# Three edits on a one-core hybrid block: the delta stage's spread and state order, a stick step that takes two heads, and the last output tile in two halves of columns

## The chip, the cores and the metric

The kernel runs on one core of one Trainium2 chip. The metric is the device time of one execution in microseconds. Of the kernel before there are three timed runs and one profiled execution. All times below are of that profiled execution, counted from the start of its span, unless something else is said.

## The reference

The program is one forward pass over a sequence of 512 positions with 1024 channels: a first block (a gated delta layer, a feed-forward layer, a banded attention layer, a second feed-forward layer, a final norm) and a second block with two branches that are gated, added and projected. Everything is float32. The parts that matter here:

```
# delta layer, per head, chunks of 64 (the kernel takes chunks of 128, four of them)
m = where(strict, (k*beta) @ k.T * decay, 0)
uw = triangular_solve(m + eye, concat([v*beta, k*beta*exp(gcum)]))     # the "solve"
v_new = u - w @ state;  o = q_dec @ state + attn_qk @ v_new
state = state * chunk_decay + k_end.T @ v_new                          # the "state" steps
o = rmsnorm(o, out_norm_w) * silu(z);  out = o @ w_out

# stick-breaking attention of the second block: 8 heads of 64, per block of queries
z = q @ k.T * dh**-0.5
log_keep = where(before, log_sigmoid(-z), 0)
log_stick = reverse_cumsum(log_keep) - log_keep
w = where(before, exp(log_sigmoid(z) + log_stick), 0);  o = w @ v      # and later o * silu(gate)

# spatial gating: 8 groups of 64 channels, chunks of 128 positions
mixed = einsum('gts,bnsgc->bntgc', w, vn) + b_s;  out = u * mixed

# the end
h = h + merged @ w_out_2;  result = rmsnorm(h, final_norm_g_2)
```

## The kernel before

Activations lie transposed: 128 channels on the partitions, 512 positions along the columns, eight such tiles for the 1024 channels (`h`). A dense product of one 128-channel output tile is 24 matmuls of 512 columns: for each of eight channel tiles k, the weights' high part with the input's high part (line 590), with its low part (line 591), and the weights' low part with the high part (line 592); in the delta stage these are called strips (line 616). The parts come about so: SyncE loads a weight tile into one of four raw slots, ScalarE casts it to the high part (`cast`, line 1152), VectorE subtracts that from the raw tile for the low part (`low`, line 1682) and so frees the slot. TensorE waits for the low part of a tile before its first matmul. The order on each engine is written out by hand, with a counting semaphore for each kind of event; every engine executes its list in order.

**Delta stage**, eight heads, one loop body each (`delta`, on TensorE, ScalarE and VectorE). A body has two halves. In the first (`levels`) TensorE multiplies a block system ("spread", line 721), ScalarE copies it out (`system_of`, line 1305), VectorE solves it (`solve`, lines 1852 to 1865) and transposes the result to `tn` (line 1872); then come four levels (products at lines 739 to 743 and, after VectorE's mask `xm`, joins at lines 756 to 760; VectorE's work in the gaps is `between(0)` to `between(7)`), with strips of tiles 2 and 3 of head i in between. In the second half four state steps t follow (lines 790 to 810; VectorE's `rr`, line 1946, and `state`, line 1961; ScalarE's `vn`, line 1330), with strips of tiles 0 and 1 of head i + 1 in between. After them VectorE normalizes k, takes the Gram product (`gram`, ending with the system's operand at line 1844), scales the outputs of head i (`outputs_of`, lines 1994 and 1997), takes the z tile of the next head and solves its system. The convolution taps (`conv_newest` on ScalarE, `conv_older` on VectorE) and silus of head i + 1 are spread over the body.

**Stick stage.** Four pairs of heads i; for each pair, each head e and each key block k (3 down to 0, with (4 - k) * 128 query columns) there is one unit, 32 in all. TensorE: logits (line 1017, full 128-row contraction: the q of one head has zeros in the other head's 64 rows), suffix sums (line 1042), values (line 1029, full 128-column weights: a head's v has zeros in the other's 64 columns). ScalarE: copy from PSUM (line 1552), exp and ln of -|z| (1557, 1559), exp of the log weight (1564). VectorE: |z| (2218), subtraction of the suffix sums (2223), mask (2226), max and add (2232), keep mask (2234), the last rows of the sum so far (2237). A step s holds the logits of unit s, the suffix sum of unit s - 2, the values of unit s - 4, and three dense pieces (a piece is one k of a tile, three matmuls) of the next pair's k, v, q tiles or of the gating stage's first tiles. 96 pieces lie inside the loop.

**Gating stage.** Four bodies; in each eight small products at line 1067 write 64 output partitions: first the four chunks of one group to partitions 0 to 63, then the four of the other to 64 to 127.

**The end.** The out stage has two bodies of four tiles. After the last tile VectorE adds it to `h` (2039), ScalarE squares it (1407), TensorE sums over channels with two f32 matmuls (1139, 1141), ScalarE takes ln and exp (1196, 1198), VectorE multiplies the eight tiles by gain and 1/rms (2385), and SyncE stores each (494).

## Time and profile before

| | us |
|---|---|
| median of three runs | 1811.98 (1811.54 to 1814.11) |
| the profiled execution | 1811.66 |
| its span, first to last instruction | 1810.0 |
| TensorE busy / VectorE busy / ScalarE busy | 1770.5 / 1188.5 / 843.6 |
| delta stage, roughly | 45 to 370 |
| stick loop | 1434 to 1558 |
| gating stage | 1558 to 1640 |
| out stage and end | 1745 to 1810 |

TensorE's granted clock is 0.999 over the span, its 2.4 GHz level. The shown durations of matmuls run from first column in to last result out and overlap; what a matmul costs in a full row of them is the time from its start to the next one's start. An f32 matmul appears as two records of equal shape; the dense products, on operands split in two parts, as one record each.

### The profile page before, as it was taken

The numbers are of one execution on the slowest core, as the hardware profiler recorded it, in microseconds if no ns is written. First come the engines' busy times: TensorE is split into PE (matmuls) and PEld (weight loads), VectorE is DVE, ScalarE is ACT, GpSimd is POOL, SyncE is SP. The second block draws the span as 40 slices with busy tenths as digits, with TensorE's granted clock in tenths as the row PEclk, the third lists the DMA queues.
The fourth block names the chain that finished last, engine by engine and source line by source line (L and its number), as shares of the span: only waits on it lengthen the run. The fifth ranks groups of instructions, "written<-read, shape, count | busy, mean of one in ns | idle before, by whom it ended". The sixth has DMA issues, their size and how long they took to land.

```text
span 1810.0 us, 23712 instructions
## 1 busy us (share of the span) xinstructions
PE 1770.5 (98%) x8122; PEld 1403.4 (78%) x8122; DVE 1188.5 (66%) x1948; ACT 843.6 (47%) x1360; POOL 35.6 (2%) x65
## 2 busy tenths in 40 slices
PE   9999999999999999999999999999999999999997
PEld 6777777678888888888887788888887876777885
DVE  7888888657777743367777677776433588765444
ACT  6554454444444432267777444444323455643222
POOL 1000000000000000000000000000001000000000
PEclk9999999999999999999999999999999999999999
DMA  5521212122222242143332222222321312323221
GB/s 201 161 69 63 65 58 60 46 82 93 93 93 93 70 144 96 62 122 100 111 100 81 94 93 93 93 93 89 117 96 52 105 36 70 97 73 99 98 93 58
DMA packets 44825, 163.27 MB, mean 90 GB/s; under 512 B 5873, under 2 KB 6148, under 8 KB 44768
## 3 DMA queue, kind: packets, MB, share of 16 engines
q1 hardware_dynamic: 39872, 148.00, 24.4%
q0 software_dynamic: 4464, 14.47, 2.9%
q8 instruction: 32, 0.52, 0.1%
q14 instruction: 25, 0.20, 0.0%
q10 hardware_dynamic: 432, 0.07, 0.0%
HBM read 155.89 MB, written 6.63 MB: 90 GB/s over the span
## 4 chain that ended last, share of the span: by engine, by line
PE 90%; DVE 5%; ACT 2%; issue 1%; DMA 0%; SPq 0%; DVEq 0%; ACTq 0%
PE acc L590 23%; PE acc L591 23%; PE acc L592 23%; PE acc L616 7%; DVE wsplit L1682 1%; PE pb L739 1%; PE pc L756 1%; PE pd L1029 1%; PE pa L1017 1%; ACT wsplit L1152 1%; PE pa L591 1%; PE pa L590 1%; PE pa L592 1%; PE pa L715 1%; PE pd L967 1%
## 5 line engine op out<-in xcount | busy, mean ns | idle before, releaser
L590 PE MATMUL acc<-xhi,wsplit 128*128 128x512 f32 x1200 | 496.6, 414 | 1.1 <-DVE at_vs L2114 1.0
L1152 ACT ACTIVATE wsplit<-wraw 128x1024 fp32r<-128x1024 f32 (+1 forms) x252 | 276.2, 1097 | 435.6 <-PE acc L592 407.9
L591 PE MATMUL acc<-xlo,wsplit 128*128 128x512 f32 x1200 | 475.5, 396 | 0.0
L592 PE MATMUL acc<-xhi,wsplit 128*128 128x512 f32 x1200 | 475.3, 396 | 0.0
L1682 DVE TENSOR_TENSOR wsplit<-wraw,wsplit 128x1024 fp32r<-128x1024 f32 (+1 forms) x249 | 316.8, 1273 | 142.4 <-ACT wsplit L1152 141.4
L590 PEld LDWEIGHTS acc<-xhi,wsplit 128*128 128x128 f32 x1200 | 226.1, 188 | 60.2 <-issue 5.3
L591 PEld LDWEIGHTS acc<-xlo,wsplit 128*128 128x128 f32 x1200 | 226.4, 189 | 55.4 <-issue 4.3
L592 PEld LDWEIGHTS acc<-xhi,wsplit 128*128 128x128 f32 x1200 | 225.8, 188 | 54.7
L616 PE MATMUL acc<-xhi,wsplit 128*128 128x512 f32 x464 | 159.1, 413 | 5.8 <-DVE wsplit L1682 5.7
L591 PE MATMUL acc<-hid_lo,wsplit 128*128 128x512 f32 x352 | 139.6, 396 | 0.0
L590 PE MATMUL acc<-hid_hi,wsplit 128*128 128x512 f32 x352 | 139.5, 396 | 0.0
L592 PE MATMUL acc<-hid_hi,wsplit 128*128 128x512 f32 x352 | 139.5, 396 | 0.0
L616 PEld LDWEIGHTS acc<-xhi,wsplit 128*128 128x128 f32 x464 | 83.9, 189 | 26.4 <-issue 9.8
L2073 DVE TENSOR_TENSOR tmp<-acc,rstd 128x512 f32<-128x512 f32 x88 | 60.5, 688 | 65.5 <-PE acc L592 57.7
L2039 DVE TENSOR_TENSOR h<-h,acc 128x512 f32<-128x512 f32 (+1 forms) x38 | 26.1, 687 | 112.4 <-PE acc L592 112.3
L616 PE MATMUL acc<-xlo,wsplit 128*128 128x512 f32 x232 | 98.8, 426 | 0.0
L1441 ACT ACTIVATE hid_hi<-fy 128x512 f32 (+1 forms) x44 | 27.8, 633 | 110.0 <-DVE fy L2084 110.0
L1434 ACT ACTIVATE fy<-tmp,vec 128x512 f32<-128x512 f32 x88 | 71.1, 809 | 17.0 <-DVE tmp L2073 17.0
L592 PEld LDWEIGHTS acc<-hid_hi,wsplit 128*128 128x128 f32 x352 | 66.3, 188 | 16.2
L590 PEld LDWEIGHTS acc<-hid_hi,wsplit 128*128 128x128 f32 x352 | 66.3, 188 | 16.2
L591 PEld LDWEIGHTS acc<-hid_lo,wsplit 128*128 128x128 f32 x352 | 66.3, 188 | 16.2
L2079 DVE SCALAR_TENSOR_TENSOR fy<-tmp,vec,fy 128x510 f32<-128x510 f32 x88 | 66.0, 750 | 12.0 <-DVE fy L2076 3.1
(386 smaller groups left out, 2611.2 us busy)
## 6 DMA issues: line engine op xcount, KB each, us to landing
wraw<-w SPq DMA_DIRECT2D x220, 512.0 KB, 3.3
wraw<-w SPq DMA_DIRECT2D x32, 704.0 KB, 4.1
bias_dram<-ext_dram POOLq DMA_DIRECT2D x1, 4096.0 KB, 23.2
bias<-bias_dram POOLq DMA_DIRECT2D x16, 256.0 KB, 3.0
at_ks<-at_ks SPq DMA_DIRECT2D x16, 256.0 KB, 2.9
crow<-row_dram POOLq DMA_DIRECT2D x8, 256.0 KB, 3.9
brow<-row_dram POOLq DMA_DIRECT2D x8, 256.0 KB, 4.5
outT<-h SPq DMA_DIRECT2D x8, 256.0 KB, 2.1
```

What stands on the lines that cost most here:

```text
L590: mm(out, whi[:, k, :], a[:, x_at + k, :], start=(k == first), stop=False)
L591: mm(out, whi[:, k, :], b[:, x_at + k, :], start=False, stop=False)
L592: m = mm(out, wlo[:, k, :], a[:, x_at + k, :], start=False, stop=(k == last))
L616: d = mm(bank(s, i, j), w[:, k, :], x[:, k, :], start=(m == 0), stop=(m == 3 * KD - 1))
L715: m = mm(pa[:, t // 2, (t % 2) * 2 * P:(t % 2 + 1) * 2 * P], kn[:, t * P:t * P + P], kq[:, t, :, :].rearrange("p a q -> p (a q)"), start=T ...
L1152: A(split(s, i, j, 0), raw(s, j), ACT.Copy).then_inc(w_hi_ready, 1)
L1434: A(fy[:, j, :], tmp[:, j % 2, :], ACT.Identity, scale=w[:, g, f, 2:3], bias=wb[:, g, f, :]).then_inc(ev("ffn_newest"), 1)
L1441: A(hid_hi[:, f, :], fy[:, j, :], ACT.Copy).then_inc(ev("hid_hi_ready"), 1)
L1682: tt_(split(s, i, j, 1), raw(s, j), split(s, i, j, 0).bitcast(F32), ALU.subtract).then_inc(w_lo_ready, 1)
L2039: tt_(h[:, i * per + m, :], h[:, i * per + m, :], bank(s, i, j) if s in rolling else acc[:, m % 2, :], ALU.add).then_inc(acc_free, 1 if s. ...
L2073: tt_(tmp[:, j % 2, :], acc[:, j % 2, :], rstd[:], ALU.mult).then_inc(acc_free, 1)
L2079: stt(fy[:, j, 2:S], tmp[:, j % 2, 0:S - 2], w[:, g, f, 0:1], fy[:, j, 2:S], ALU.mult, ALU.add).then_inc(ev("ffn_conv"), 1)
```

## The change

- **Delta, TensorE:** `spread(i + 1)` moves from the start of the next body to the end of this one, six strips ahead of its end (for the last head the order of TensorE stays).
- **Delta, VectorE:** `outputs_of` is cut in two; its second multiply (`outputs_normed`) moves behind `solve(i + 1)`. `low(i + 1, 0)` moves from gap 7 to gap 6, the last tap of tile 2 from gap 6 to gap 7; the taps of tile 3 and `exponent` move later in the state steps.
- **Delta, ScalarE:** the cast of the outputs (`output_hi`) moves into the next body, behind the first weight cast; `square_k` and `conv_newest(3)` move behind `vn_of(0)`. Head 0 is unrolled.
- **Stick, all engines:** a step takes both heads of a block: 16 blocks instead of 32 units. Logits are two 64-row products into two PSUM banks, values two 64-column products into two partition halves; `sk_q` and `sk_vt` lose their zero halves, and GpSimd its memsets. ScalarE and VectorE operations span both heads. |z| moves to ScalarE; the mask is added before |z|, so the keep mask is gone. Dense pieces: six a step up to step 10, then the rest over seven steps.
- **Gating, TensorE:** the eight products alternate between the two halves.
- **End:** the last tile is computed in two halves of 256 columns; the norm's sum, root, multiplies and stores are done by halves, the multiplies of four and three tiles in one instruction. The gain is multiplied in earlier, tile by tile. The loops of the out stage are unrolled.

```diff
# TensorE, delta
             def levels(i, last):
-                if last:
-                    out_pieces(*OUT_SPREAD)
-                spread(i)
...
-                    fill((3 * KD if last_qkv else 2 * 3 * KD) - done[0])
+                    whole = 3 * KD if last_qkv else 2 * 3 * KD
+                    fill(whole - done[0] - (0 if last_qkv else AFTER_SPREAD))
+                    if last_qkv:
+                        out_pieces(*OUT_SPREAD)
+                    spread(i + 1)
+                    fill(whole - done[0])
# VectorE, delta
-                    if gap in (4, 5, 6):
+                    if gap in (4, 5):
                         conv_older(i, 2, i + 1, (gap - 3,))
+                    if gap == 6:
+                        low(s, i + 1, 0)
                     if gap == 7:
-                        low(s, i + 1, 0)
+                        conv_older(i, 2, i + 1, (3,))
                         take(i, 3)
...
-                if not last:
-                    conv_older(i, 3, i + 1, (1,))
...
                         if t == 1 and not last:
-                            conv_older(i, 3, i + 1, (3,))
-                            exponent(i + 1)
+                            conv_older(i, 3, i + 1, (2, 3))
...
                         if t == 0 and not last:
-                            conv_older(i, 3, i + 1, (2,))
+                            conv_older(i, 3, i + 1, (1,))
+                        if t == 1 and not last:
+                            exponent(i + 1)
...
-                    outputs_of(i)
-                    dve.wait_ge(ev("oy_ready"), i + 1)
+                    outputs_gated(i)
+                    dve.wait_ge(ev("on_ready"), i + 1)
                     take(i + 1, 0)
                     solve(i + 1)
+                    outputs_normed(i)
# ScalarE, delta
                 if not last:
                     cast_ahead(s, i, 1, False)
+                if not (isinstance(i, int) and i == 0):
+                    output_hi(i - 1)
+                if not last:
                     conv_newest(1, i + 1, i)
...
-                    square_k(i)
-                    conv_newest(3, i + 1, i)
...
                 vn_of(0)
                 if not last:
+                    square_k(i)
+                    conv_newest(3, i + 1, i)
# TensorE, stick
+                        for e in range(2):
+                            own = slice(64 * e, 64 * e + 64)
+                            m = mm(pa[:, e, 0:(4 - k) * P], sk_k[own, i % 2, k * P:k * P + P], sk_q[own, i % 2, k * P:S],
+                                   start=True, stop=True)
+                        m.then_inc(ev("logits_done"), 1)
+                    a = done + (upto(step) - done + 1) // 2
+                    c = a + (upto(step) - done) // 6
+                    dense(done, a)
+                    if 1 <= step < blocks + 1:
+                        k = 3 - (step - 1) % NC
+                        pe.wait_ge(ev("sp_ready"), step)
...
+                        for e in range(2):
+                            m = mm(pbc[:, e, 0:(4 - k) * P], order[:, O_SUF, :], sp[:, e, SEG[k]:SEG[k] + (4 - k) * P],
+                                   start=True, stop=True)
+                        m.then_inc(ev("suffix_done"), 1)
+                    dense(a, c)
+                    if step >= 2:
+                        i, k = (step - 2) // NC, 3 - (step - 2) % NC
+                        pe.wait_ge(ev("sw_ready"), step - 1)
...
+                        for c0, c1 in zip(cuts, cuts[1:]):
+                            for e in range(2):
+                                own = slice(64 * e, 64 * e + 64)
+                                m = mm(pd[own, c0 * P:c1 * P], sk_vt[:, i % 2, k, own],
+                                       sw[:, e, SEG[k] + (c0 - k) * P:SEG[k] + (c1 - k) * P], start=(k == 3), stop=(k == 0 and c1 == NC))
# ScalarE, stick: order of a step
+                    if step < blocks:
...
+                        A(zs[:, :, g], pa[:, :, 0:(4 - k) * P], ACT.Copy).then_inc(ev("zs_ready"), 1)
+                    if 2 <= step < blocks + 2:
...
+                        A(sw[:, :, g], zs[:, :, g], ACT.Exp).then_inc(ev("sw_ready"), 1)
+                    if step < blocks:
...
+                        A(sw[:, :, g], zs[:, :, g], ACT.Abs).then_inc(ev("z_abs"), 1)
+                        A(sw[:, :, g], sw[:, :, g], ACT.Exp, scale=-1.0).then_inc(ev("z_exp"), 1)
+                        A(sw[:, :, g], sw[:, :, g], ACT.Ln, bias=1.0).then_inc(ev("z_ln"), 1)
+                    if 0 < i < SBP and v == 0:
+                        turned_v(i)
+                        cast_ahead(s, i, 2, i == SBP - 1)
+                    if i < SBP - 1 and v in (1, 3):
+                        cast_ahead(s, i + 1, v // 2, i + 1 == SBP - 1)
# VectorE, stick: order of a step
+                        tt_(zs[:, :, g], zs[:, :, g], pbc[:, :, 0:(4 - k) * P], ALU.subtract).then_inc(ev("drest"), 1)
...
+                        x = stt(sp[:, :, g], zs[:, :, g], 0.0, sw[:, :, g], ALU.max, ALU.add)
...
+                            x = stt(sp[LAST:P, :, later], pbc[0:32, :, 0:(3 - k) * P], cst[LAST:P, C_ID, LAST:LAST + 1],
+                                    sp[LAST:P, :, later], ALU.mult, ALU.add)
...
+                        tt_(zs[:, :, own], zs[:, :, own], order[:, O_NEGD, :].unsqueeze(1).to_broadcast([P, 2, P]), ALU.add
+                            ).then_inc(ev("z_masked"), 1)
+                    if ahead and v == 3:
                         take(i + 1, 2)
...
+                    if ahead and v in (1, 2):
+                        take(i + 1, v - 1)
+                    if ahead and v in (2, 3):
+                        low_ahead(s, i + 1, v - 2, i + 1 == SBP - 1)
# TensorE, gating
-                    for e in range(2):
-                        for t in range(NC):
+                    for t in range(NC):
+                        for e in range(2):
# TensorE, end
+                product(s, j, acc[:, 1, 0:HALF], a, b, 0, KD).then_inc(acc_done, 1)
+                a, b = mg_hi[:, :, HALF:S], mg_lo[:, :, HALF:S]
+                product(s, j, pb[:, 0:HALF], a, b, 0, 5)
+                final_sum(0)
+                product(s, j, pb[:, 0:HALF], a, b, 5, KD).then_inc(acc_done, 1)
+                final_sum(1)
# VectorE, end
+                for k0, k1 in FINAL_PARTS:
+                    if k1 < KD:
+                        x = tt_(h[:, k0:k1, cols], h[:, k0:k1, cols], rstd[:, cols].unsqueeze(1).to_broadcast([P, k1 - k0, HALF]), ALU.mult)
+                    else:
+                        x = stt(h[:, k0, cols], h[:, k0, cols], vec[:, G_FIN2 + k0:G_FIN2 + k1], rstd[:, cols], ALU.mult, ALU.mult)
# SyncE, end; FINAL_PARTS = [(0, 4), (4, 7), (7, 8)]
+            for n in range(2):
+                for m, (k0, k1) in enumerate(FINAL_PARTS):
...
+                    sp.dma_start(outT[part], h[part]).then_inc(ev("stored"), 16)
```

## Rows read from the trace of the kernel before

**Rows 1.** The page's first part: busy us, share of the span, instructions of each engine.
```profile
PE 1770.5 (98%) x8122; PEld 1403.4 (78%) x8122; DVE 1188.5 (66%) x1948; ACT 843.6 (47%) x1360; POOL 35.6 (2%) x65
```
**Rows 2.** TensorE's waits: us in total, times, longest us.
```profile
PE acc L616 <- DVE wsplit L1682: 5.7, 7, 0.8
PE pb L739 <- DVE tn L1872: 5.7, 8, 1.0
```
**Rows 3.** Timeline of TensorE in one head: start us, duration us, instruction, idle before.
```profile
173.04 0.60 PE L721 MATMUL pa<-xm,cst 128*128 128x256 f32 x2
...
176.75 0.40 PE L616 MATMUL acc<-xlo,wsplit 128*128 128x512 f32 x1
177.89 1.16 PE L739 MATMUL pb<-tn,gd 128*128 128x128 f32 x8 [0.74 <-DVE tn L1872]
...
193.94 0.49 PE L616 MATMUL acc<-xhi,wsplit 128*128 128x512 f32 x1 [0.82 <-DVE wsplit L1682]
...
213.64 0.60 PE L721 MATMUL pa<-xm,cst 128*128 128x256 f32 x2
```
**Rows 4.** Timeline of VectorE in the same head.
```profile
174.11 0.31 DVE L1852 TENSOR_TENSOR st<-system 128x144 f32<-128x144 f32 x1 [0.56 <-ACT system L1305]
...
192.26 0.42 DVE L1937 COPY tt<-pd 64x256 f32<-64x256 f32 x1
...
195.42 0.75 DVE L1752 SCALAR_TENSOR_TENSOR ys<-tmp,vec,ys 128x511 f32<-128x511 f32 x1 [1.01 <-ACT ys L1235]
...
211.61 0.43 DVE L1844 TENSOR_TENSOR xm<-gdc,en 128x256 f32<-128x256 f32 x1
```
**Rows 5.** Timeline of TensorE: start, one step and end of the stick loop.
```profile
1434.27 0.60 PE L1003 MATMUL acc<-cst,sk_v 128*128 128x128 f32 x4
...
1488.38 1.02 PE L1017 MATMUL pa<-sk_q,sk_k 128*128 128x512 f32 x2
...
1489.47 0.39 PE L591 MATMUL acc<-xlo,wsplit 128*128 128x512 f32 x1
...
1558.39 0.60 PE L1054 MATMUL pb<-cst,gv 128*128 128x128 f32 x4
```
**Rows 6.** Groups by line and shape, 1430 to 1562 us: busy us, mean ns; idle before.
```profile
L1682 DVE TENSOR_TENSOR wsplit<-wraw,wsplit 128x1024 fp32r<-128x1024 f32 x13 | 15.9, 1225 | 0.6 <-ACT wsplit L1152 0.3
...
L1152 ACT ACTIVATE wsplit<-wraw 128x1024 fp32r<-128x1024 f32 x13 | 13.6, 1047 | 4.6 <-PE acc L592 4.6
...
L2218 DVE SCALAR_TENSOR_TENSOR sw<-zs 128x512 f32<-128x512 f32 x8 | 5.5, 692 | 1.8 <-ACT zs L1552 1.7
...
L1557 ACT ACTIVATE sw<-sw 128x512 f32<-128x512 f32 x8 | 5.0, 628 | 0.0
...
L2218 DVE SCALAR_TENSOR_TENSOR sw<-zs 128x128 f32<-128x128 f32 x8 | 2.3, 290 | 4.5 <-ACT zs L1552 4.5
```
**Rows 7.** Timeline of TensorE around one gating product.
```profile
1569.60 0.39 PE L591 MATMUL acc<-xlo,wsplit 128*128 128x512 f32 x1
1569.83 0.40 PE L592 MATMUL acc<-xhi,wsplit 128*128 128x512 f32 x1
1570.16 1.58 PE L1067 MATMUL pc<-wcur,xc 128*64 128x128 f32 x16
1571.67 0.50 PE L590 MATMUL acc<-xhi,wsplit 128*128 128x512 f32 x1
1572.00 0.40 PE L591 MATMUL acc<-xlo,wsplit 128*128 128x512 f32 x1
```
**Rows 8.** Line 1067 by windows: stretch, length, TensorE busy (records touching it), clock, DMA.
```profile
1570.90:1571.00 0.10, 0.10 (x7) 1.00 0.00 0
```
**Rows 9.** Timeline of VectorE at the end.
```profile
1797.98 0.69 DVE L2039 TENSOR_TENSOR h<-h,acc 128x512 f32<-128x512 f32 x1 [3.48 <-PE acc L592]
...
1801.99 5.39 DVE L2385 SCALAR_TENSOR_TENSOR h<-h,vec,rstd 128x512 f32<-128x512 f32 x8 [3.32 <-ACT rstd L1198]
```
**Rows 10.** The page's DMA issues: count, KB each, median us to landing.
```profile
outT<-h SPq DMA_DIRECT2D x8, 256.0 KB, 2.1
```

294 lines of the change are left out of this document (133 added, 161 removed).

## The prediction

> **What bounds the kernel now.** I read the page's busy list first: TensorE has work for 98% of the span, VectorE for 66% [rows 1]. So only three things can shorten the run: fewer TensorE column cycles, less waiting of TensorE, or a shorter tail behind its last product. Then the list of waits: almost all that TensorE waits for in the delta stage are two VectorE results, about 0.7 us a head each, the turned blocks tn ahead of line 739 and the low half of a weight tile ahead of line 616 [rows 2]. The timeline of one head (its period is 213.64 - 173.04 = 40.6 us) places them [rows 3]. A dense matmul takes 0.235 us from start to start [rows 7], so between 176.75 and 177.89 us 0.90 us are lost; the wait before 193.94 is shown as 0.82 and costs some 0.16 more by the same reading, 0.98. Next the stick stage: from 1434.27 to 1558.39 us, 124.1 us [rows 5]. It holds 96 dense pieces of three matmuls, 67.5 us; 96 f32 products for logits, suffix sums and values, each at 0.43 us a record of 512 columns, two records a matmul (two records and one dense step fill the 1.09 us from 1488.38 to 1489.47 [rows 5]): 32 head-blocks x 320 columns on average x 1.68 ns = 17.1 us per kind, 51.2 in all; transposes 1.8; rest, some 3.6 us, waits. It is TensorE's stage, though VectorE is close behind. Last the end: 12 us behind the last product [rows 9].
>
> **Delta: the spread six matmuls earlier, the outputs' last multiply behind the solve.** The spread for the next head now stands 6 x 0.235 = 1.41 us before the old place, at 212.23 us in a head where it stood at 213.64 [rows 3]. Its operand is finished at 211.61 + 0.43 = 212.04 [rows 4], so TensorE does not wait for it, with 0.2 us to spare. The solve waited 0.56 us for the copy of the spread [rows 4]; it now starts 1.4 us earlier, because one 0.69 us multiply is gone from before it. tn is then ready 0.5 us before TensorE wants it: the 0.90 us go. What comes late next is the moved multiply and the low half, ahead of the first level's mask on VectorE; by the same durations they end within 0.1 us of when its operand is there. I take nothing for it. Head 0's solve stays as it was, and the last head's spread keeps its place, so it is 6 heads x 0.90 = 5.4 us. The output cast on ScalarE now stands behind the next head's weight cast; behind it there waits only the newest tap of tile 1, whose input VectorE gives after the first level's mask, later than the cast ends. It costs nothing unless the moved multiply slips behind that mask; then all 0.69 us of it would show in each head.
>
> **Delta: the low half before the last join.** The 1.23 us subtraction goes from behind the copy at 192.26 [rows 4] into the gap before it; it ends at about 192.5, half a microsecond before TensorE's two strips of the next tile, and the copy is needed only after those. The 0.98 us go. In exchange one 0.75 us tap of tile 2 moves behind it, and its silu stands before the first vn on ScalarE: 0.1 us. The newest tap of tile 3 moves behind vn; VectorE, which waited 1.01 us for it before 195.42 [rows 4], gets it later and holds up rr by 0.15 to 0.3. Price 0.2, bounds 0 and 0.7 (all of that tap). Net 0.78 x 7 heads = 5.5 us. The two delta edits give 10.9, bounds 7 and 12.5.
>
> **Stick: two heads a step.** What is removed on VectorE (|z|, the keep mask, half of the instruction starts, one of two q multiplies) takes it from near 28 us a pair of heads to 18, each operation priced at its columns by rows 6; |z| goes to ScalarE, which stays near 19 us. Both are below TensorE's 30. Neither gain is on the path by itself.
>
> On TensorE the logits of two heads contract over 64 rows each, in different halves of the array, and the values go to different halves of the output partitions. Do these run at once? The trace has one such case: line 1067 writes partitions 0 to 63 eight times, then 64 to 127 eight times. 16 records of 0.107 us of columns should fill 1.71 us, but the next dense matmul starts 1.51 us after the first [rows 7], though it pays for two changes. And in the table by tenths of a microsecond seven records are in flight in the middle [rows 8], where a start every 0.107 us and a duration of 0.27 allow three or four: the second half of the array starts while the first still works. So column halves overlap, even out of program order. For row halves the trace shows nothing; the bounds are full overlap and none, and I take full overlap from that nearest row. Logits and values each go from 17.1 to 8.5 us: -17.1.
>
> The Trainium skill, "TensorE: Matmul & The Clock Gate" (section "The mechanism"), has matmuls start and end in strict program order. The measured overlap contradicts that for column halves; by that rule the two records of the second head would start only with the second of the first.
>
> The same excursion has a price. Line 1067 starts 0.33 us after the dense matmul before it, where 0.235 is usual, and behind it the second dense matmul comes 0.33 after the first [rows 7]: 0.19 us outside the group. Inside its 1.51 us I estimate 0.14 for a slow first record and the way back: 0.33 us in all. Full-array excursions (line 1017, rows 5) cost none. The change makes 32 excursions, two a block: +10.7 us, bounds 0.19 and 0.5 each, 6 and 16.
>
> The Trainium skill, "TensorEngine Tiling (Array Packing)" (section "Key Properties"), says that changing the tiling mode drains the engine; the trace agrees with its 0.33 us.
>
> Then the chain of one step. DVE's durations follow 0.16 us + 1.05 ns a column [rows 6], so both heads at 512 columns cost 1.23, at 384 0.95; ScalarE's likewise 1.08. Take the widest block (v = 3), TensorE's step beginning at 0: logits 1.2, copy to 2.4, exponential of an older block to 3.0, |z|, exp and ln to 6.3. Now ScalarE's weight cast (1.05 [rows 6]) to 7.3, for which VectorE's low half waits, to 8.6, and behind which stand the subtraction for the older block (9.6), this block's sum and its wrap-around rows, to 11.9. TensorE asks for it at 10.2: its step is 4.2 dense + 1.2 + 1.3 + 0.8 = 7.5, then 0.5 of logits and 2.1 dense. It stalls 1.7 us, in three of the four pairs: +5.1, bounds 0 (the low half is ready early) and 9. The waits at the end, 3.6 us, I leave. Sum: 124.1 - 17.1 + 10.7 + 5.1 = 122.8: only 1.3 us gained.
>
> **Gating, order of the eight products.** Alternating halves run from the start at one record in 0.109 us per half: 0.87 + 0.2 instead of 1.51: 0.44 x 4 = 1.8 us; bounds 0 and 2.6.
>
> **The end.** The last tile in halves costs TensorE nothing but the f32 sum (0.43 + 0.43 a half). Before, from the last addition at 1797.98 to the first final multiply at 1801.99 4.01 us pass, and the eight multiplies take 5.39 [rows 9]. After, the second half's addition stands at 1798.9, since the first half's sum (0.86) is put before its last nine products; the same chain at half the columns takes about 2.9 us, to 1801.8; the first half's multiplies (1.23 + 0.95 + 0.42) fit in between. The second half's three end at 1804.4 instead of 1807.4: 3.0. The seven extra multiplies by the gain lie in VectorE's idle time in the out stage. The stores now have 1 KB runs and fewer, larger pieces. 256 KB took 2.1 us to land [rows 10]; the last pieces come at 1 MB in 1.3 us, so I take 0.4 off: 2.6 us, bounds 0.5 and 3.2.
>
> **Sum.** 10.9 + 1.3 + 1.8 + 2.6 = 16.6. VectorE fills 86% of a shorter head afterwards, and ends that I put within 0.1 to 0.2 us of each other will not all hold; for that I take off 1.6. 1811.66 (the profiled execution, span 1810.0) - 15 = 1796.7; its median of three is 0.3 above, so 1797.0. About 0.2% (3.6 us) is what a measurement can tell from no change.
>
> **Rivals.**
> - Row halves don't overlap. For it: no row shows 64-row products. Against: rows 8 for columns. The logits keep 17.1 us: +8.5, of which about 2 fall into stalls that exist anyway: 1803.5. Chance 0.13.
> - Starts in program order. Then a head pair's four records take three slots: the logits save 4.3 instead of 8.5, the values (cut in two pieces) 5.6: +7.2, less 1 of stalls: 1803. Rows 7 and 8 speak against it. Chance 0.04. (It is the rule of the Trainium skill cited above.)
> - New waits eat half of the delta gain, because VectorE, not TensorE, then sets the head's period: +5.4: 1802.4. For it: 0.2 us margins; against: 14% idle VectorE. Chance 0.12.
> - Cheap excursions and a short chain: if the stall of 5.1 does not come and an excursion costs 0.25: -7.7: 1789.5. Chance 0.09.
> - Slower: the excursion is dearer for row halves. All other gains together are 15 us; 16 logits excursions decide from 0.33 + 15/16 = 1.3 us each. At 1.7 us, if each time the array had to run empty and two weight loads followed in series, +22: 1819. Nothing in the rows is near it. Chance 0.02.
> - The change doesn't do what it says (waits reappear one for one, stick as before): within 0.2%. Chance 0.02.
>
> The forecast keeps 0.58, own range 1793 to 1801. The whole range, 1790 to 1804, takes in the first three rivals. Faster by over 0.2%: 0.96, same 0.02, slower 0.02.
>
> **What will show it.** Right: no wait for tn at line 739 in heads 1 to 6 and none for a weight tile at 616; a head's period of 38.9 us; stick loop between 120 and 126 us with waits of TensorE for sp once in a pair; lines 1067's group under 1.1 us; pa's two halves starting together; last multiply ending near 1790. Wrong: second-head logits starting after the first's (row halves), a period still above 40 us (VectorE-bound), or stick below 117 (my stall is not there).

## The result and the profile after

The changed kernel takes 1793.74 us (median of four runs, 1793.58 to 1794.55); the kernel before, timed beside it on the same chip, 1811.88 (1811.54 to 1814.11). The ratio is 0.9899, with a 95% interval of 0.9886 to 0.9911: 18.1 us less. The forecast was 1797.0 with a range of 1790 to 1804. The profiled execution has a span of 1791.9 us; all times inside a run are counted from its start.

The first part of the page, as [rows 1], and TensorE's longest waits in the delta and stick stages and at the end, as [rows 2] (us in total, times, longest us):

```profile
PE 1761.8 (98%) x8174; PEld 1388.8 (78%) x8174; DVE 1153.6 (64%) x1826; ACT 845.8 (47%) x1311; POOL 34.4 (2%) x61
```
```profile
PE pbc L1029 <- DVE sp L2263: 4.5, 4, 1.8
...
PE pbc L792 <- DVE rr L1976: 1.1, 4, 0.4
PE pbc L1147 <- ACT tmp L1699: 1.1, 1, 1.1
PE pbc L733 <- DVE tn L1902: 1.0, 1, 1.0
```

The wait for a weight tile's low half (5.7 us in [rows 2]) is gone, and of the waits for tn only head 0's is left. A wait for sp, the tile that the suffix sums read, takes the first place; the list of before has none. The old stick loop had another:

```profile
PE pd L1029 <- ACT sw L1564: 2.5, 3, 1.0
```

It is gone too.

Where the 18.1 us come from, by the start of the stick loop (its first transpose, line 1003 before and 1002 now) and the stages behind it:

| stage | before | after | less |
|---|---|---|---|
| up to the stick loop | 1434.27 | 1422.23 | 12.0 |
| stick loop | 124.12 | 121.48 | 2.6 |
| gating product, each of 4 | 1.51 | 1.03 | 1.9 in all |
| from the last gating product's start to the end | 181.5 | 180.0 | 1.5 |

**Delta.** TensorE's timeline at two spreads one head apart: the period is 205.68 - 167.03 = 38.65 us, where [rows 3] gives 40.6.

```profile
166.79 0.40 PE L613 MATMUL acc<-xhi,wsplit 128*128 128x512 f32 x1
167.03 0.59 PE L718 MATMUL pa<-xm,cst 128*128 128x256 f32 x2
167.27 0.58 PE L613 MATMUL acc<-xhi,wsplit 128*128 128x512 f32 x1
167.69 0.40 PE L613 MATMUL acc<-xlo,wsplit 128*128 128x512 f32 x1
...
205.68 0.59 PE L718 MATMUL pa<-xm,cst 128*128 128x256 f32 x2
```

**Stick.** TensorE's timeline over the widest block of a pair and the first of the next, to be held against [rows 5]:

```profile
1471.11 0.40 PE L589 MATMUL acc<-xhi,wsplit 128*128 128x512 f32 x1
1471.44 1.13 PE L1017 MATMUL pa<-sk_q,sk_k 64*128 64x512 f32 x4
1472.50 0.50 PE L587 MATMUL acc<-xhi,wsplit 128*128 128x512 f32 x1
1472.84 0.40 PE L588 MATMUL acc<-xlo,wsplit 128*128 128x512 f32 x1
...
1481.81 0.39 PE L589 MATMUL acc<-xhi,wsplit 128*128 128x512 f32 x1
1483.28 1.98 PE L1029 MATMUL pbc<-sp,order 128*128 128x512 f32 x4 [1.08 <-DVE sp L2263]
```

The logits of two heads are four records of 512 columns, and the next dense matmul follows 1.06 us after the first of them. Full overlap of two row halves takes 0.85 for the columns (two records at 0.43). In the trace's records the four start at 1471.438, 1471.445, 1471.971 and 1471.978: two at a time, 0.007 us apart. The last line is a stall: from 1481.81 a dense matmul accounts for 0.23 of 1.47 us. The first matmuls behind the logits also lie 0.34 us apart instead of 0.235, as in [rows 7].

What holds sp up stands in VectorE's timeline of the same moment:

```profile
1474.91 0.69 DVE L2238 SCALAR_TENSOR_TENSOR sk_q<-acc,rstd 128x512 f32<-128x512 f32 x1 [0.81 <-PE acc L589]
1478.35 1.23 DVE L1712 TENSOR_TENSOR wsplit<-wraw,wsplit 128x1024 fp32r<-128x1024 f32 x1 [2.75 <-ACT wsplit L1170]
1479.49 0.68 DVE L2293 TENSOR_TENSOR ya_lo<-sk_o,ya_hi 128x512 fp32r<-128x512 f32 x1
1480.10 0.95 DVE L2253 TENSOR_TENSOR zs<-zs,pbc 128x768 f32<-128x768 f32 x1
1480.96 1.22 DVE L2258 SCALAR_TENSOR_TENSOR sp<-zs,sw 128x1024 f32<-128x1024 f32 x1
1482.21 1.01 DVE L2263 SCALAR_TENSOR_TENSOR sp<-pbc,cst,sp 32x768 f32<-32x768 f32 x1
```

VectorE stands 2.75 us at the low half (line 1712), waiting for ScalarE's cast, with four operations queued behind it; the last releases TensorE at 1483.2.

**Gating**, TensorE, against [rows 7]: the group of 16 records lasts 1.03 us to the next dense matmul instead of 1.51.

```profile
1555.47 1.09 PE L1071 MATMUL pbc<-wcur,xc 128*64 128x128 f32 x16
1556.50 0.51 PE L587 MATMUL acc<-xhi,wsplit 128*128 128x512 f32 x1
```

**The end**, VectorE, against [rows 9]: second half's addition, the first half's multiplies, the second half's.

```profile
1782.31 0.42 DVE L2419 TENSOR_TENSOR h<-h,pbc 128x256 f32<-128x256 f32 x1 [3.29 <-PE pbc L589]
1782.65 2.08 DVE L2427 TENSOR_TENSOR h<-h,rstd 128x1024 f32<-128x1024 f32 x2
...
1785.52 2.09 DVE L2427 TENSOR_TENSOR h<-h,rstd 128x1024 f32<-128x1024 f32 x2 [0.39 <-ACT rstd L1217]
1787.53 0.48 DVE L2429 SCALAR_TENSOR_TENSOR h<-h,vec,rstd 128x256 f32<-128x256 f32 x1
```

The last multiply ends at 1788.0, and the span 3.9 us later; before, 2.6 us lay between them (1801.99 + 5.39 = 1807.4 [rows 9], span 1810.0). In the kernel before the DMA engines were already full at that place. By window (last two columns: their share, GB/s), from the second multiply on:

```profile
1804.00:1809.00 5.00, 0.00 (x0) 0.00 (x0) 3.38 (x6) 0.00 (x0) 0.00 (x0) 0.57 1.02 381
```

### The profile page after: what moved, and what is told of

Read it like the earlier page. It is cut to its first block, busy times and chain, and to the rows that moved or that the text cites. A ratio compares the mean times of both kernels' runs of the same rounds, so it can differ in the third digit from the quotient of the medians.

```text
span 1791.9 us, 23591 instructions
## 1 busy us (share of the span) xinstructions
PE 1761.8 (98%) x8174; PEld 1388.8 (78%) x8174; DVE 1153.6 (64%) x1826; ACT 845.8 (47%) x1311; POOL 34.4 (2%) x61
## 4 chain that ended last, share of the span: by engine, by line
PE 91%; DVE 4%; ACT 3%; issue 1%; DMA 0%; SPq 0%; DVEq 0%; ACTq 0%
PE acc L587 23%; PE acc L588 23%; PE acc L589 23%; PE acc L613 8%; ACT wsplit L1170 1%; PE pbc L750 1%; PE pbc L954 1%; PE pbc L733 1%; PE pa L587 1%; PE pa L588 1%; PE pa L589 1%; DVE wsplit L1712 1%; PE pbc L1029 1%; PE pa L712 1%; PE pd L967 1%
## 5 line engine op out<-in xcount | busy, mean ns | idle before, releaser
L2077 DVE TENSOR_TENSOR h<-h,acc 128x512 f32<-128x512 f32 (+2 forms) x38 | 25.8, 680 | 107.2 <-PE acc L589 107.2
```

The lines of the kernel that those rows point to most:

```text
L2077: tt_(h[:, i * per + m, cols], h[:, i * per + m, cols], out, ALU.add).then_inc(acc_free, 1 if s.kc == KD else 2)
```

## The experiments

Twelve kernels ran, in three groups of four (e1 to e4, e5 to e8, e9 to e12), each group on another chip and timed beside the kernel before (1811.91, 1812.11 and 1812.39 us). The changed kernel had 1811.88 beside it. So a difference between kernels of different groups is known to some 0.5 us; measured against the kernel before of its own group, e7 is -0.24, e9 -0.29, e10 +2.76, e11 -0.60 and e12 +3.07. The loop is the stick loop of the profiled execution.

| run | base | median us (all runs) | against its base | loop starts | loop lasts |
|---|---|---|---|---|---|
| changed kernel | | 1793.74 (1793.58 to 1794.55) | | 1422.23 | 121.48 |
| e1_delta_back | changed | 1805.89 (1805.61 to 1807.11) | +12.15 | 1434.46 | 121.50 |
| e2_stick_back | changed | 1796.37 (1795.84 to 1796.47) | +2.63 | 1422.33 | 124.10 |
| e3_low_late | changed | 1799.48 (1799.20 to 1801.34) | +5.74 | 1429.97 | 121.50 |
| e4_spread_back | changed | 1800.75 (1800.59 to 1801.24) | +7.01 | 1428.71 | 122.67 |
| e5_low_behind_sp | changed | 1789.15 (1788.73 to 1789.31) | -4.59 | 1422.31 | 116.90 |
| e6_logits_whole | changed | 1797.01 (1796.81 to 1797.17) | +3.27 | 1422.19 | 124.90 |
| e7_store_out | changed | 1793.73 (1793.31 to 1795.40) | -0.01 | | |
| e8_gate_end_back | changed | 1797.16 (1796.93 to 1797.30) | +3.42 | 1422.32 | 121.47 |
| e9_finer_parts | changed | 1793.96 (1793.21 to 1795.06) | +0.22 | 1422.02 | 122.72 |
| e10_values_whole | e5 | 1792.19 (1791.68 to 1793.91) | +3.04 | 1421.83 | 120.10 |
| e11_best | e5 | 1788.83 (1788.55 to 1788.86) | -0.32 | 1422.31 | 116.73 |
| e12_two_visits | e5 | 1792.50 (1792.41 to 1794.06) | +3.35 | 1423.85 | 120.38 |

### The delta edit: whole, and its two pieces

**e1_delta_back** puts the three engines' old delta order back (spread at the head of `levels`, `low(s, i + 1, 0)` in gap 7, both outputs' multiplies ahead of the solve, the old order between the state's steps) and nothing else; it holds the two diffs below, on ScalarE the old places of the output cast, `square_k` and tile 3's newest tap, and, on VectorE (with the first of these taps back ahead of the state steps),

```
                         if t == 1 and not last:
-                            conv_older(i, 3, i + 1, (2, 3))
+                            conv_older(i, 3, i + 1, (3,))
+                            exponent(i + 1)
...
                         if t == 0 and not last:
-                            conv_older(i, 3, i + 1, (1,))
+                            conv_older(i, 3, i + 1, (2,))
```

> The changed kernel with the old delta order throughout (spread at the head of levels, the low part of strip 0 in the last gap of the levels, old order between the state's steps, o_hi taken in its own iteration); stick step, gating and end stay changed. Theory, the delta edit is a gain of its own in the 8-head loop and nothing behind it depends on it: the stick loop starts 12.0 us later (at 1434.3 instead of 1422.2), the stages behind it keep their lengths (121.5, 1.03 x4, 16.4), and the time is 1793.7 + 12.0 = 1805.8. Rival, part of the 12.0 came from the later stages' earlier loads or from the buffers: the stick loop starts less than 10 us later.

The loop starts at 1434.46, the time is +12.15, and the loop behind lasts 121.50. The theory holds: the delta edit is worth 12.1 us by itself, and nothing behind it hangs on it.

**e3_low_late**:

```
-                    if gap in (4, 5):
+                    if gap in (4, 5, 6):
                         conv_older(i, 2, i + 1, (gap - 3,))
-                    if gap == 6:
-                        low(s, i + 1, 0)
                     if gap == 7:
-                        conv_older(i, 2, i + 1, (3,))
+                        low(s, i + 1, 0)
                         take(i, 3)
```

> The changed kernel with one piece of the delta edit undone: in the levels, VectorE's low part of strip 0 goes back from the sixth gap (ahead of the last join's read) to the seventh (behind it), and the last convolution of q ahead of it. Theory, the low part released late cost TensorE 0.98 us a head before the first strip of the next head, and is worth its wait less 0.1: about 7 x 0.9 = 6.3 us more, 1800.0, and the wait on the low part at the strip (line 613) is back at about 1 us per head. Rival, the spread's shift and the new order between the state's steps already give the low part the time: under 2 us more, 1795.

+5.74, and the wait is back to the figure: TensorE's list has

```profile
PE acc L613 <- DVE wsplit L1712: 5.7, 7, 0.8
```

as in [rows 2]. (Its loop starts 7.7 us later in the profiled execution, because 1.9 us of that are lost ahead of the first spread: there the granted clock fell for some 3 us, as the last section shows. From the first spread to the last product of the output projection it is 5.8 us longer.)

**e4_spread_back** moves the spread and VectorE's last multiply of the output back:

```
     def levels(i, last):
+        if last: out_pieces(*OUT_SPREAD)
+        spread(i)
...
-        fill(whole - done[0] - (0 if last_qkv else AFTER_SPREAD))
-        ...
-        spread(i + 1)
-        fill(whole - done[0])
+        fill((3 * KD if last_qkv else 2 * 3 * KD) - done[0])
...
-        outputs_gated(i); take(i + 1, 0); solve(i + 1); outputs_normed(i)
+        outputs_of(i);    take(i + 1, 0); solve(i + 1)
```

> The changed kernel with the other piece of the delta edit undone: the spread matmul stands again at the head of levels, with nothing between it and the level's first product but that head's 14 strip matmuls, and VectorE multiplies the output by its norm ahead of the solve. Theory, the wait of 0.9 us on tn at the first level product is back, about 6 x 0.9 = 5.4 us, plus the 0.24 per head that the strips paid behind the spread, 1.7: 1799 to 1801. If both pieces add up, the rises of this run and of the run with the low part late sum to 12.0 within 1. Rival, one of the two waits covers the other: the two rises sum to under 9.

+7.01. TensorE's timeline of one head:

```profile
169.93 0.40 PE L613 MATMUL acc<-xhi,wsplit 128*128 128x512 f32 x1
170.16 0.60 PE L718 MATMUL pa<-xm,cst 128*128 128x256 f32 x2
170.72 0.50 PE L613 MATMUL acc<-xhi,wsplit 128*128 128x512 f32 x1
171.06 0.39 PE L613 MATMUL acc<-xlo,wsplit 128*128 128x512 f32 x1
...
173.87 0.40 PE L613 MATMUL acc<-xlo,wsplit 128*128 128x512 f32 x1
175.01 1.16 PE L736 MATMUL pbc<-tn,gd 128*128 128x128 f32 x8 [0.75 <-DVE tn L1899]
```

The 0.90 us ahead of the level product are back (175.01 - 173.87 - 0.24), and a second cost shows that the forecast had not read: from the spread to the second strip behind it 0.90 us pass here (170.16 to 171.06), and 0.66 in the changed kernel (167.03 to 167.69). That is 0.24 a head. 6 x (0.90 + 0.24) = 6.8. The two pieces add up to 12.75, 0.6 more than e1, which also puts the order between the state steps and ScalarE's order back; that third part has no run of its own. Where the 0.24 us come from is open. The tile that follows the spread is another (strips of tiles 2 and 3 before, of tiles 0 and 1 now), and the edge of the loop body stood right ahead of the spread and now lies among strips; no run changed either alone.

### The stick step

**e2_stick_back** takes the old stick code on all four engines, with its padded `sk_q` and `sk_vt`:

```
-                for step in range(blocks + 2):
+                for step in range(units + 4):
...
-                            m = mm(pa[:, e, 0:(4 - k) * P], sk_k[own, i % 2, k * P:k * P + P], sk_q[own, i % 2, k * P:S],
+                        mm(pa[:, u % 2, 0:(4 - k) * P], sk_k[:, i % 2, k * P:k * P + P], sk_q[:, i % 2, e, k * P:S],
```

> The changed kernel with the old stick step: one head per step, 34 logits and values over all 128 rows of zero-padded operands, mask added behind the subtraction, no whole-step order change elsewhere. Theory: the stick loop goes back from 121.5 to 124.1 us and the rest keeps its length: 1793.7 + 2.6 = 1796.3. Rival, the row halves save more than the loops' own lengths show, because the old loop began with other loads in flight: a loop other than 124.1 by over 1 us.

+2.63, loop 124.10. (The text says "34 logits and values"; there are 32 of each, one a head and block.) The stick gain is 2.6 us, independent of the other edits. Three runs take it apart.

**e5_low_behind_sp**, on VectorE:

```
-                    if ahead and v in (2, 3):
-                        low_ahead(s, i + 1, v - 2, i + 1 == SBP - 1)
+                    if ahead and v == 2:
+                        low_ahead(s, i + 1, 0, i + 1 == SBP - 1)
                     if 0 < i < SBP and v == 0:
+                        low_ahead(s, i, 1, i == SBP - 1)
                         low_ahead(s, i, 2, i == SBP - 1)
```

> The changed kernel with one move on VectorE: the low part of the next pair's second tile (line 1712, which waits 2.75 us for ScalarE's cast with the subtraction and sp queued behind it) goes from the last step of a pair to the next step, behind sp and the mask. Theory, that order makes the whole stall at the suffix of the widest block: the waits of TensorE on sp (0.64, 1.24 and 1.95 us between the pairs) vanish, the stick loop is 121.5 - 3.8 = 117.7 us, the time 1793.7 - 3.8 = 1789.9. Rival, the stall is the chain's own (ScalarE's three functions and the subtraction end as late without the low part): under 1 us less. Second rival, the low part becomes late for TensorE's dense products, a wait of 1 us or more at lines 587 to 589 in each of two pairs: 1791.5 to 1792.

-4.59, loop -4.58. TensorE at the place of the stall above:

```profile
1481.16 0.39 PE L589 MATMUL acc<-xhi,wsplit 128*128 128x512 f32 x1
1481.39 1.88 PE L1029 MATMUL pbc<-sp,order 128*128 128x512 f32 x4
```

No gap is left, at this pair and the two others, and of the 4.5 us of waits for sp one is left, at the last block:

```profile
PE pbc L1029 <- DVE sp L2263: 1.2, 1, 1.2
```

So the order of one VectorE instruction made the whole stall between the pairs; both rivals fall. The gain is 0.8 above the sum of the three stalls: the suffix product behind each is 0.10 us shorter when TensorE did not stand before it (1.31 instead of 1.42 to the next dense matmul), and two small waits of 0.2 in the last pair's steps go too. Without the stall the loop is 7.2 us shorter than the old one (124.1 to 116.9), so the stall was a cost of the new step itself.

**e6_logits_whole** gives the logits 128 rows again:

```
-            own = slice(64 * e, 64 * e + 64)
-            m = mm(pa[:, e, ...], sk_k[own, i % 2, ...], sk_q[own, i % 2, k * P:S], ...)
+            m = mm(pa[:, e, ...], sk_k[:, i % 2, ...], sk_q[:, i % 2, e, k * P:S], ...)
```

> The changed kernel with the logits alone back to 128 rows of zero-padded q (both heads one after the other, in the array's whole mode), the values still in halves of columns. It tells the overlap of the row halves from the price of a change of mode. The overlap is worth 4 x (0.21 + 0.43 + 0.64 + 0.85) = 8.5 us in the traces. Theory, each of the 16 visits to row halves costs 0.39 us, 6.2 in all, and the stall shrinks by some 0.6 as the steps grow: 1793.7 + 8.5 - 6.2 - 0.6 = 1795.4. With the forecast's 0.33 per visit: 1796.3. Rival, the excess beside the logits comes from elsewhere (the waits, the values' mode), and the row halves change mode for nothing: 1793.7 + 8.5 = 1802.

+3.27, loop +3.42, 1.6 us above the theory's time. Below, a visit is one change from whole-array matmuls to halves and back, what the prediction calls an excursion. The block of the timeline above reads here

```profile
1472.24 0.39 PE L593 MATMUL acc<-xhi,wsplit 128*128 128x512 f32 x1
1472.47 1.88 PE L1020 MATMUL pa<-sk_q,sk_k 128*128 128x512 f32 x4
1473.79 0.79 PE L591 MATMUL acc<-xhi,wsplit 128*128 128x512 f32 x1
1474.42 0.40 PE L592 MATMUL acc<-xlo,wsplit 128*128 128x512 f32 x1
```

From the dense matmul ahead to the second one behind: 2.18 us (1472.24 to 1474.42), against 1.73 (1471.11 to 1472.84) in halves. The halves save 0.45 of the 0.85 us that their columns save. The same difference at 384, 256 and 128 columns is 0.24, 0.03 and -0.18, a loss at the narrowest: 0.54 a pair, 2.2 for the four. So a visit of row halves costs (8.5 - 2.2) / 16 = 0.39 us against whole rows. The same lines give its bare price: 1.73 less two dense starts (0.47) and 0.85 for columns is 0.40 in halves (from 1.726), and 2.18 - 0.47 - 1.71 is 0.00 whole. The other 1.2 us of the loop are waits: those at the three pair boundaries grow from 0.6, 1.2 and 1.9 us by 0.50 each, the one at the last block shrinks by 0.25. The expectation had taken them to shrink. VectorE takes q in two instructions of 64 rows, 1.39 us instead of 0.69, and the same chain starts later. The rival without a price for the mode (1802) falls.

That two halves work at once shows in windows of 0.1 us (stretch, length, TensorE busy and in brackets the records that touch it): inside the logits of 512 columns, the changed kernel has

```profile
1471.90:1472.00 0.10, 0.10 (x4) 0.00 (x0) 0.00 (x0) 0.00 (x0) 0.00 (x0) 1.00 0.00 0
```

and e6, in the middle of the same group, where the heads follow each other,

```profile
1473.30:1473.40 0.10, 0.10 (x2) 0.07 (x1) 0.00 (x0) 0.00 (x0) 0.00 (x0) 1.00 0.00 0
```

**e10_values_whole**, on e5: the values of a head go to all 128 output partitions from padded v, one head after the other; logits stay in halves.

```
-                                m = mm(pd[own, c0 * P:c1 * P], sk_vt[:, i % 2, k, own], ...)
+                                m = mm(pd[:, c0 * P:c1 * P], sk_vt[:, e, i % 2, k, :], ...)
```

> On the kernel with the low part behind sp (1789.15, no stalls between the pairs): the values back to whole columns with zero-padded v (head by head), the logits still in row halves. The step of 0.21 us per 128 columns says that the column halves overlap fully; whole they cost 4 x (0.21 + 0.43 + 0.64 + 0.85) = 8.5 us more, and 16 visits to the halves' mode less. Theory, a visit costs 0.39: + 8.5 - 6.2 = 2.3, so 1791.5. Rival, the column halves change mode for nothing: + 8.5, 1797.6. As with the logits, short matmuls in the whole mode can hide some of their start beside the dense ones: then up to 1 us less.

+3.04, loop +3.20. By the same sum a visit of column halves costs (8.5 - 3.04) / 16 = 0.34 us against whole columns (0.33 by the loop). Median and theory are 0.7 apart, within what the runs' spread (1791.68 to 1793.91) and the two groups leave; the rival at 1797.6 falls.

**e12_two_visits**, on e5: one dense product goes between the two cuts of the values.

```
                         for c0, c1 in zip(cuts, cuts[1:]):
+                            if c0 > k:
+                                dense(c, c + 1)
+                                c += 1
                             for e in range(2):
```

> On the kernel with the low part behind sp (1789.15): in the 12 blocks whose values stand in two cuts of columns, one dense product of three matmuls goes between the cuts, so that the array changes to column halves and back 12 times more, with not one matmul added. Theory, each visit to a half mode costs 0.39 us whatever is done in it: 12 x 0.39 = 4.7, so 1793.8. With the forecast's 0.33: 1793.1. Rival, the excess belongs to the matmuls in halves (a start of their own each) and not to the change of mode: no change, 1789.2.

+3.35, loop +3.48. TensorE:

```profile
1478.36 0.39 PE L589 MATMUL acc<-xhi,wsplit 128*128 128x512 f32 x1
1478.68 0.44 PE L1045 MATMUL pd<-sw,sk_vt 128*64 128x128 f32 x4
1479.05 0.50 PE L587 MATMUL acc<-xhi,wsplit 128*128 128x512 f32 x1
1479.38 0.40 PE L588 MATMUL acc<-xlo,wsplit 128*128 128x512 f32 x1
```

From 1478.36 to 1479.38 there are two dense starts (0.47) and 128 columns in overlapped halves (0.21); 0.34 us are the visit's own. No matmul was added, so the price belongs to the change between whole array and halves, and the rival (a price of each matmul in halves) falls. Twelve such visits are 4.1 us; 3.5 arrive in the loop, because one falls into the wait ahead of the last suffix (1.33 in e5, 0.99 here, from dense start to suffix less 0.23) and one is part hidden.

### Gating and the end

**e8_gate_end_back** has the old loops there: gating head by head, the last tile whole, one sum, eight multiplies and eight stores of whole rows.

```
-                    for t in range(NC):
-                        for e in range(2):
+                    for e in range(2):
+                        for t in range(NC):
...
-            for half in range(2):
-                ...
+            for k in range(KD):
+                stt(h[:, k, :], h[:, k, :], vec[:, G_FIN2 + k:G_FIN2 + k + 1], rstd[:], ALU.mult, ALU.mult)
```

> The changed kernel with the old order in gating (head by head instead of chunk by chunk) and the old end (the output's last tile whole, one sum of squares, eight multiplies by gain and norm, eight stores of whole rows). The two are read apart by their stages. Theory: the product of gating goes from 1.03 to 1.51 us in each of 4 pairs, +1.9, and from the last tile's first matmul to the end 16.35 becomes 17.84, +1.5: 1793.7 + 3.4 = 1797.1. Rival, in gating the 0.48 us is taken back by the wait that follows: the stage grows by less than 1 us, and the time is under 1796.

+3.42. From the first gating transpose to the last gating product 70.07 us instead of 68.13: +1.94; from there to the end 181.5 instead of 180.0: +1.5. The rival in gating falls. VectorE at the old end:

```profile
1787.41 5.39 DVE L2393 SCALAR_TENSOR_TENSOR h<-h,vec,rstd 128x512 f32<-128x512 f32 x8 [3.32 <-ACT rstd L1200]
```

The last multiply ends at 1792.80, the span at 1795.4. Less the 2.0 us by which this run comes late at the addition's stage, the halves bring the last multiply 2.8 us forward and give 1.3 back behind it.

**e7_store_out** leaves out the first of the six stores:

```
                     sp.wait_ge(ev("final_ready"), ...)
-                    sp.dma_start(outT[part], h[part]).then_inc(ev("stored"), 16)
+                    if n + m > 0:
+                        sp.dma_start(outT[part], h[part]).then_inc(ev("stored"), 16)
```

> The changed kernel without its first store: tiles 0 to 3 of the output's first half of columns (1 MB / 4 x 2 = 0.5 MB of the 2 MB) are never written to outT; all arithmetic stays. Theory, behind the last multiply the DMA engines set the end (3.9 us from the last multiply to the end, where before 2.6): with a quarter of the bytes gone the queue is no longer full there, and the end comes up to 1.3 us earlier, 1792.4 to 1793.0, with 2.6 to 3.2 us behind the last multiply. Rival, the 3.9 us are the landing time of half-width rows or of three stores issued one after the other: no change within 0.3 us, 1793.7.

1793.73: no change that can be told (the profiled span is 0.2 us shorter). The theory as I put it, a backlog that alone sets the end, falls. By windows (last two columns: share of the DMA engines, GB/s), first the changed kernel, then e7:

```profile
1785.00:1788.00 3.00, 0.00 (x0) 0.00 (x0) 2.61 (x4) 0.38 (x1) 0.00 (x0) 0.62 1.03 340
1788.00:1791.00 3.00, 0.00 (x0) 0.00 (x0) 0.00 (x1) 0.00 (x0) 0.00 (x0) 0.50 1.01 340
```
```profile
1787.00:1788.00 1.00, 0.00 (x0) 0.00 (x0) 1.00 (x2) 0.00 (x0) 0.00 (x0) 0.50 0.57 193
1788.00:1791.00 3.00, 0.00 (x0) 0.00 (x0) 0.00 (x0) 0.00 (x0) 0.00 (x0) 0.50 0.94 315
```

Without the backlog the engines have free time at 1787, and yet they are busy nearly as long in the last 3 us: the second half's first store is issued only at 1786.8, behind a multiply over four tiles, and 1 MB (1024 KB in three stores) at 340 GB/s is 3.1 us.

**e9_finer_parts**:

```
-FINAL_PARTS = [(0, 4), (4, 7), (7, 8)]
+FINAL_PARTS = [(0, 1), (1, 4), (4, 7), (7, 8)]
```

> The changed kernel with the multiplies and stores of the end in parts (0,1), (1,4), (4,7), (7,8) instead of (0,4), (4,7), (7,8), in both halves. Theory, from the run without the first store: the end has two limits that lie 0.3 us apart, the backlog of the whole 2 MB at 340 GB/s from the first store (6.1 us), and 1 MB at that rate from the second half's first store (3.1 us), and both go with how early a first store is issued. The first store of each half is now issued after one tile (0.4 us) instead of four (1.2 us): the end 0.6 to 0.8 us earlier, 1793.7 - 0.7 = 1793.0. Rival, the last store's own landing sets the end, and one more multiply in each half makes it later by 2 x 0.15: 1794.0.

1793.96, with runs from 1793.21 to 1795.06: no gain that can be told. From the last product's last matmul (1783.01 here, 1781.99 in the changed kernel) to the end there are 9.6 us instead of 9.9. Only the first 128 KB leave early; the DMA engines then stand partly idle until the store of the next three tiles (a share of 0.44 from 1785 to 1786, 1.03 in the next us), and the 6 us at 340 GB/s start where they did. The expected 0.7 treated all of the bytes as if they could leave with the first store.

**e11_best** joins e5, the finer parts and, in the stick step, ScalarE's `ya_hi` behind the logarithm and VectorE's `ya_lo` behind the next sp:

```
+                    if 7 <= step < blocks and v == 3:      # ScalarE, behind Ln instead of ahead of the copy
+                        A(ya_hi[:, n, :], sk_o[:], ACT.Copy)
...
-                    if step >= 7 and v == 3 or step == blocks + 2:      # VectorE
+                    if step >= 8 and v == 0 or step == blocks + 2:
```

> The version meant to beat both: the low part behind sp, the finer parts at the end, and ScalarE's ya_hi behind the logarithm of the last block (VectorE's ya_lo behind sp of the next step), so that the copy of the last block's logits starts 0.5 us earlier and the wait of 1.43 us ahead of the last suffix becomes 0.9. Theory: 1789.15 - 0.7 - 0.5 = 1787.9. Rival, the last block's wait is bound by ScalarE's three functions and not by when its copy starts, and the stores' gain fails: 1789.2.

1788.83, ratio to the kernel before 0.9868 (0.9851 to 0.9884), and 0.32 under e5 (0.60 when each is measured against the kernel before of its group). The wait ahead of the last suffix falls from 1.33 to 0.85 (0.5, as expected; the expectation's 1.43 reads the same wait 0.1 longer), but two waits of 0.1 and 0.2 in the steps before it grow, and the stores' part is 0.3 at most. It beats both kernels; nearly all of its lead over the changed kernel is the one VectorE instruction of e5.

## Why the prediction was right

The sign and the range hold, and so do the mechanisms of the delta, stick and gating edits; at the end it misread what bounds the stores. The time lies 3.3 us under the forecast. Of these 1.6 are the allowance for unforeseen waits, and 1.5 the terms: 1.2 in delta, 1.3 in stick and 0.1 in gating too small, 1.1 at the end too large. That the terms miss by so little in sum is in part luck: the end's error works against the others, and inside the stick term errors of 1.0 and 1.6 us offset each other.

- **Delta, 10.9 forecast, 12.1 measured** (e1). The low half ahead of the last join: 5.5 against 5.7 (e3). The spread: 5.4 against 7.0 (e4). The step that was too small is the second: it priced only the wait for tn and not the 0.24 us a head that the strips behind the spread lose at the old place. The 0.1 us margins mostly held. One wait of TensorE for VectorE grew, that for rr: 0.4 us in two places before (line 798), 1.1 in four now.
- **The 1.6 us taken off for unforeseen waits** were not lost in delta. Without them the forecast would have been 1795.4. The rival in which VectorE sets the head's period (40 us and over) falls with a period of 38.65, of which VectorE is busy 33.8 us (87%, 86% forecast).
- **Stick, 1.3 forecast, 2.6 measured.** Term by term: the overlap of both kinds of halves, -17.1, is full (e6, e10 and the four records in flight). By the Trainium skill, "TensorE: Matmul & The Clock Gate" (section "The mechanism"), matmuls start in strict program order; the trace does not agree. With that order the logits of 512 columns would need three slots of 0.43 us, 1.3; measured are 1.06, half of the visit's price included. The old gating order shows it without that sum: its trace holds two series of eight records, 0.109 us from start to start, one from 1570.16 and one from 1570.65, when three of the first series have not started. (Which half a record belongs to isn't written in the trace; two starts 0.006 us apart can't be in one half, where the columns take 0.107.) Between the two logits matmuls as wholes the order is kept: each record of the second starts 0.007 us behind its fellow of the first. The 32 visits: 10.7 against 16 x 0.39 + 16 x 0.34 = 11.7. The bare price of column halves read in e12, 0.34, is the forecast's 0.33, which came from column halves; row halves cost 0.40, some 0.06 more, and that was not foreseen. The stall: 5.1 against 3.8 at the three boundaries, 4.6 with all that e5 removed, and by the very chain that the forecast had written out. The sum -17.1 + 11.7 + 4.6 is -0.8 and the loop lost 2.6: most of the rest is the step "the waits at the end, 3.6 us, I leave". It was wrong. From start to start, less what the instruction ahead takes, the old loop has three waits for sw (1.11, 0.78 and 1.07 us, 3.0 in all), and the new one a single wait for sp at its last block, 1.33. That is 1.6 less, and -2.4 in all; 0.2 us stay open.
- **Gating, 1.8 forecast, 1.9 measured** (e8): right, from the one row of the old group's overlap.
- **The end, 2.6 forecast, 1.5 measured** (e8). The multiplies come 2.8 us earlier (3.0 forecast). The term that was mis-sized is the stores: 0.4 us taken off, 1.3 lost. The forecast let the end follow the last multiply by a landing time. But the DMA engines were full from 1804 to 1809 in the kernel before, so what counted was when the first store left and at what rate. In the changed kernel the first store waits for four tiles, 1.24 us behind the start of the first multiply instead of 0.77 (1782.65 to 1783.89, 1801.99 to 1802.76), and the 2 MB take 6.3 us from the first packet to the last instead of 5.6: 0.5 + 0.7 is 1.2 of the 1.3. These are read from the two traces and not tested one by one; e7 and e9 show that the second half's first store, at 1786.8, is a second limit, 0.2 to 0.3 us behind.
- **Rivals.** Of "cheap excursions and a short chain" (1789.5) only the second half can be had: the excursions are not cheap, but the stall can be removed, and e5 stands at 1789.15. That the two times agree is chance.

## What to carry to other kernels

When an edit makes another engine's chain critical, look in that engine's timeline for the instruction with a long wait ahead of the critical one in its queue: here moving one subtraction by half a step gave more (4.6 us) than the whole new stick step had with its stall (2.6). Packing two 64-row or 64-column products into halves of the array pays only by the columns: against whole-array matmuls each visit costs 0.39 us for row halves and 0.34 for column halves, which here is more than the saving at 128 columns and most of it at 256. And before a tail is split, look whether the stores already fill the DMA engines there: then the end moves with the first store and the rate, not with the last multiply.

## What the runs showed of the hardware beside that

- **Halves out of order.** Product groups that alternate between halves of the array run at twice the rate of columns (gating: 16 records in 1.03 us, where one half after the other took 1.51), without any change of the instructions but their order.
- **Rows of 1 KB in the output cost rate.** The stores ran at 340 GB/s in the halves. Before, at eight stores of whole 2 KB rows, the DMA engines moved 364 to 394 GB/s in the slices of the same stage, and e8, with whole rows again, 364 to 400. The size of a store isn't the cause: the stores of e9 have 128 and 384 KB where the changed kernel's have up to 512, at the same 340.
- **The clock can fall behind a wait.** In the profiled execution of e9 TensorE waits 1.78 us for sp, and the four suffix records behind take 3.67 us instead of 1.99. By windows (after POOL's column stands the granted clock):

```profile
1511.00:1513.00 2.00, 0.51 (x3) 0.07 (x1) 1.97 (x3) 0.84 (x1) 0.00 (x0) 1.00 0.57 217
1513.00:1515.00 2.00, 1.71 (x2) 0.73 (x3) 0.66 (x2) 1.21 (x4) 0.00 (x0) 0.61 0.00 0
1515.00:1517.00 2.00, 2.00 (x5) 0.45 (x5) 0.50 (x1) 1.47 (x3) 0.00 (x0) 0.54 0.00 0
1517.00:1519.00 2.00, 2.00 (x15) 1.09 (x15) 2.00 (x3) 0.00 (x0) 0.00 (x0) 1.00 0.17 23
```

The granted clock falls from 2.4 to 1.2 GHz for some 3 us behind the wait. It did so at the same place in e4 too (both loops last 1.2 us more in the table), and in none of the other profiled executions with the same wait. In the profiled executions of e3 and e12 it fell near the start, behind a wait of 1.8 us for the first inputs (line 645); here e12:

```profile
16.00:18.00 2.00, 2.00 (x6) 1.62 (x5) 2.00 (x4) 1.86 (x3) 0.00 (x0) 0.50 1.02 405
```

The window holds six matmuls; in e11, which has the same wait, it holds ten at a granted clock of 1.00. These executions of e3 and e12 (1801.34 and 1794.06 us) are 1.8 and 1.5 us above the next of their kernels. What decides whether the clock falls stays open.
